# Two transformer blocks in fp32 on one core: evictions, weight halves and side work queued later

## What is computed

```python
def hybrid_mixer(h, pos, w_in, ...):
    z, xbc, dt_f, dt_b, q, k, v, gates = split_cols(h @ w_in, IN_SPLITS)
    xbc = silu(depthwise_centred_conv(xbc, conv_w, conv_b))          # 5 taps, 3072 channels
    xs, b_in, c_in = split_cols(xbc, (2048, 512, 512))
    ...
    y = ssd(xs, dtf, af, b_in, c_in) + flip(ssd(flip(xs), ...)) + d_skip * xs
    y = gated_group_rmsnorm(y, z, ssd_norm_g)                        # y * silu(z), 4 groups
    branch_ssd = y @ w_br_ssd
    q = rotary(q, pos); k = rotary(k, pos)
    branch_attn = windowed_gqa_with_sink(q, k, v, sink) @ w_br_attn  # 16 heads, window 128
    g_ssd, g_attn = split(sigmoid(gates))
    return (g_ssd * branch_ssd + g_attn * branch_attn) @ w_out
```

## Time and profile before

| what | value |
|---|---|
| median of three executions | 2611.15 us (2610.36 to 2611.34) |
| the profiled execution | 2610.12 us, its span 2608.3 us |
| TensorE busy | 2483.5 us (95%) |
| VectorE, ScalarE, GpSimd busy | 1327.3 us (51%), 929.5 us (36%), 477.9 us (18%) |
| mean granted TensorE clock | 0.981 |
| HBM traffic | 95 GB/s over the span |

### The profile page before, as it was taken

One profiled execution on the slowest core, in us unless ns is written; L12 is line 12 of the kernel. 1 busy time (PEld: TensorE's weight loads), 2 busy tenths in 40 slices (PEclk: granted clock), 3 DMA queues, 4 the chain that ended last, 5 costly groups with the idle time before them and its releaser, 6 DMA issues.

```text
span 2608.3 us, 29119 instructions
## 1 busy us (share of the span) xinstructions
PE 2483.5 (95%) x11378; PEld 1992.6 (76%) x11378; DVE 1327.3 (51%) x1957; ACT 929.5 (36%) x1488; POOL 477.9 (18%) x329
## 2 busy tenths in 40 slices
PE   6999899989789999999999999999999999999997
PEld 5766567867668788788888788888877787888886
DVE  3788855455776544444443344433477644444422
ACT  4334334233455433333332333322544333333321
POOL 2422100044330010111111111101355311111101
PEclk9999999989899999999999999999999999999998
DMA  5412123432344523233332233322321232333331
GB/s 162 124 57 57 41 89 135 140 97 77 101 138 143 196 97 113 73 97 97 97 97 97 81 103 97 98 97 95 93 65 57 73 113 64 92 98 97 98 102 49
DMA packets 173258, 254.20 MB, mean 97 GB/s; under 512 B 11840, under 2 KB 88896, under 8 KB 173120
## 3 DMA queue, kind: packets, MB, share of 16 engines
q1 hardware_dynamic: 173120, 252.33, 30.6%
HBM read 231.83 MB, written 16.78 MB: 95 GB/s over the span
## 4 chain that ended last, share of the span: by engine, by line
PE 76%; DVE 12%; issue 5%; ACT 4%; POOL 1%; DMA 1%; SPq 1%; DVEq 0%; ACTq 0%; POOLq 0%
PE bank L997 75%; DVE T L1716 3%; DVE W L1708 1%; POOL acc L2429 1%; ACT whi L1300 1%; DVE wlo L1708 1%; ACT pr L1392 1%; DVE pr L1712 1%; DVE T L1713 1%; DVE pr L1826 0%; PE bank L1077 0%; DMA scr_z<-T 0%; DVE SC L2343 0%; ACT T L1301 0%; DVE stg L1716 0%
## 5 line engine op out<-in xcount | busy, mean ns | idle before, releaser
L997 PE MATMUL bank<-xh,whi 128*128 128x512 f32 x1784 | 720.9, 404 | 22.0 <-DVE wlo L1708 17.6
L1708 DVE TENSOR_TENSOR wlo<-raw,whi 128x1024 fp32r<-128x1024 f32 (+1 forms) x354 | 438.9, 1243 | 570.9 <-ACT whi L1300 570.4
L997 PE MATMUL bank<-xh,wlo 128*128 128x512 f32 x1784 | 700.5, 393 | 0.0
L997 PE MATMUL bank<-xl,whi 128*128 128x512 f32 x1784 | 700.0, 392 | 0.0
L1300 ACT ACTIVATE whi<-raw 128x1024 fp32r<-128x1024 f32 (+2 forms) x406 | 416.5, 1038 | 541.6 <-PE bank L997 530.9
L997 PEld LDWEIGHTS bank<-xh,whi 128*128 128x128 f32 x1784 | 338.2, 190 | 119.5 <-issue 30.5
L997 PEld LDWEIGHTS bank<-xh,wlo 128*128 128x128 f32 x1784 | 337.5, 189 | 72.7
L997 PEld LDWEIGHTS bank<-xl,whi 128*128 128x128 f32 x1784 | 338.2, 190 | 69.3 <-issue 3.8
L997 PE MATMUL bank<-hh,wlo 128*128 128x512 f32 x528 | 205.6, 389 | 0.0
L997 PE MATMUL bank<-hl,whi 128*128 128x512 f32 x528 | 205.6, 389 | 0.0
L997 PE MATMUL bank<-hh,whi 128*128 128x512 f32 x528 | 205.6, 389 | 0.0
(11 more groups left out here) (341 smaller groups left out, 3623.5 us busy)
## 6 DMA issues: line engine op xcount, KB each, us to landing
raw<-in_w_in SPq DMA_DIRECT2D x92, 512.0 KB, 3.6
raw<-in_w_ffn_in SPq DMA_DIRECT2D x88, 256.0 KB, 3.3
raw<-in_ffn_gate SPq DMA_DIRECT2D x88, 256.0 KB, 2.8
raw<-in_ffn_up SPq DMA_DIRECT2D x88, 256.0 KB, 3.1
raw<-in_ffn_down SPq DMA_DIRECT2D x44, 512.0 KB, 3.5
raw<-in_w_ffn_out SPq DMA_DIRECT2D x22, 512.0 KB, 3.5
raw<-in_w_xattn_kv SPq DMA_DIRECT2D x16, 512.0 KB, 4.0
raw<-in_w_kv_mem SPq DMA_DIRECT2D x16, 512.0 KB, 3.8
```

Of the source, the lines that this page charges most:

```text
L997: return e.matmul(out, l, r, start=start, stop=stop, skip_group_check=skip)
L1708: return e.tensor_tensor(out, a, b, op)
```

## The change

- `gemm` no longer evicts a tile directly behind its matmuls: the eviction is put in `owed`, and paid behind the matmuls of the next tile, or at a mark, a drain or a flush.
- A slot's step is split in two: `w_hi` at the old place, `w_lo` put off with `soon(1, ...)` from the fourth slot on.
- `attention` is written anew: the evictions (`score_max`, `pt_out`, `o_out`), the shift, the exponentials and the normalisation are steps of their own, one yield or more behind what they read; its rate is 3.0 instead of 2.5.
- The copy of a turned tile (`turned`), the gates' tanh, z's product (`z_silu`), the square of the gated y (`z_square`) and the sums of the memories' squares (`m_sum`) are put off by `soon`.
- `y_add` stands first in its point. The states wait for the last read of the states of the group before (`off`, g-1, 3, 0) in place of the marks.
- The functions of the engines keep their operations; most are only renamed. The core of the diff:

```diff
@@ -308,10 +308,17 @@
 
         ORDER = []
         loaded, ready = [0], [0]
-        jobs, aged, beside, late, delayed, tails = [], [], [], [], [], []
+        jobs, aged, beside, late, delayed, tails, owed = [], [], [], [], [], [], []
 
         def step(kind, *args):
+            if kind == "mark":
+                pay()
             ORDER.append((kind, args))
+
+        def pay():
+
+            while owed:
+                owed.pop(0)()
 
         def load_to(j):
             while loaded[0] < min(j, NS):
...
@@ -321,7 +328,11 @@
         def split_to(j):
             while ready[0] < min(j, NS):
                 load_to(ready[0] + NR)
-                step("w", ready[0])
+                step("w_hi", ready[0])
+                if ready[0] < 4:
+                    step("w_lo", ready[0])
+                else:
+                    soon(1, "w_lo", ready[0])
                 ready[0] += 1
 
         def pump():
...
@@ -387,8 +403,9 @@
                     if j == 0:
                         main.new(name, m)
                     step("mm", name, j, m)
+                    pay()
                     if i == g["ids"][-1]:
-                        evict(m)
+                        owed.append(lambda m=m: evict(m))
                     if m == (g["M"] - 1) // 2:
                         pump()
                     run_beside((g["n"] if g["nat"] else g["ntok"]) / (4 * S))
...
@@ -491,31 +508,49 @@
             return max(n - 1, 0), min(n + 2, 4)
 
         def attention():
+
+
             for i in range(17):
+                here, last = i < 16, i - 1
+                k = keys(last)[1] - keys(last)[0] if i else 0
                 for pair in range(2):
-                    if i < 16:
-                        for r in (0, 1) if pair == 0 else (2, 3):
+                    if here:
+                        for r in (2 * pair, 2 * pair + 1):
                             side.new("sc", i, r)
                         step("scores", i, pair)
+                    if i > 1 and pair == 0:
+                        step("o_out", i - 2)
+                    if i and pair:
+                        step("pt_out", last, 0)
+                    yield
+                    if here:
+                        step("score_max", i, pair)
                         if pair:
-                            step("softmax", i)
-                        yield
-                    if i and pair == 0:
-                        k0, k1 = keys(i - 1)
-                        for j in range(k1 - k0):
-                            side.new("pt", i - 1, j)
-                            step("p_turn", i - 1, j)
-                            yield
-                    if i and pair:
-                        side.new("pv", i - 1)
-                        step("pv", i - 1)
-                    if pair and i < 16:
-                        step("p_norm", i)
-                    if pair:
-                        yield
+                            step("shift", i)
+                    if i:
+                        side.new("pt", last, pair)
+                        step("p_turn", last, pair)
+                    yield
+                if here:
+                    step("p_exp", i)
+                if i:
+                    step("pt_out", last, 1)
+                if k == 3:
+                    side.new("pt", last, 2)
+                    step("p_turn", last, 2)
+                    yield
+                    step("pt_out", last, 2)
+                yield
+                if i:
+                    side.new("pv", last)
+                    step("pv", last)
+                if here:
+                    step("p_norm", i)
+                yield
+            step("o_out", 15)
 
         step("mark", "qkv")
-        att = start(attention(), 2.5)
+        att = start(attention(), 3.0)
         step("conv_weights")
 
         def ev_conv(j):
...
@@ -534,6 +569,7 @@
                     def turn():
                         side.new("turn", j)
                         step("turn", j)
+                        soon(1, "turned", j)
                     return (lambda: turn()) if j < 20 else None
                 return silu
             jobs.append(conv)
...
@@ -542,7 +578,8 @@
             def evict(m):
                 tmp.new(key, base + m)
                 step("gate", key, base + m)
-                soon(1, "gate_out", key, base + m)
+                soon(1, "gate_tanh", key, base + m)
+                soon(2, "gate_out", key, base + m)
             return evict
 
         for g in range(4):
...
@@ -601,16 +638,19 @@
             g, c = posts.pop(0)
             z_there.discard((g, c))
             step("z_gate", g, c)
-            z_busy[0] -= 1
+
+            def square():
+                step("z_square", g, c)
+                z_busy[0] -= 1
+            soon(1, square)
             if c == 3:
-                soon(1, "y_mean", g)
-                soon(3, "y_scale", g)
+                soon(2, "y_mean", g)
+                soon(4, "y_scale", g)
 
 
         SEG, WITHIN, ELSE = (0, 1), (2,), (3,)
 
         def states(g):
-            step("mark", f"ssd{g}")
             for i in range(6):
                 if i == 0:
                     step("weigh", g, 0)
...
@@ -657,6 +697,10 @@
             ahead = groups(1, 4)
             for n in range(34):
                 for half in range(2):
+                    if half == 1 and n >= 2 and n % 2:
+                        step("y_add", (n - 2) // 2)
+                        if n % 8 == 1:
+                            posts.extend(((n - 2) // 8, c) for c in range(4))
                     if half == 0 and n >= 2:
                         if n % 2 == 0:
                             side.new("y", (n - 2) // 2, among=WITHIN)
...
@@ -672,10 +716,6 @@
                         step("decayed", n - 1)
                     if n % 8 >= 2:
                         next(ahead, None)
-                    if half == 1 and n >= 2 and n % 2:
-                        step("y_add", (n - 2) // 2)
-                        if n % 8 == 1:
-                            posts.extend(((n - 2) // 8, c) for c in range(4))
                     if posts and posts[0] in z_there:
                         post()
                     fetch_z()
...
@@ -686,7 +726,11 @@
                 tmp.new("z", g, m)
                 tmp.new("zt", g, m)
                 step("z_out", g, m)
-                z_done.add((g, m))
+
+                def silu():
+                    step("z_silu", g, m)
+                    z_done.add((g, m))
+                soon(1, silu)
             return evict
 
 
...
@@ -702,6 +746,7 @@
                 step("m_split", tag, k)
                 square(f"m{tag}", k)
                 soon(1, "m_lo", tag, k)
+                soon(1, "m_sum", tag, k)
                 yield
 
         def memory(tag):
...
@@ -735,8 +780,8 @@
                 step("y_turn", j)
                 if j < 15:
                     yield
-                if posts:
-                    fetch_z()
+                fetch_z()
+                if posts and posts[0] in z_there:
                     post()
             step("x_again")
 
...
@@ -1489,9 +1536,8 @@
                     return
                 to = c + 1 if d == 0 else c - 1
                 u, b = side("st", g, i)
-                w.wait_ge(*at("pe", f"ssd{g}"))
-                w.wait_ge(*at("dve", f"ssd{g}"))
-                w.wait_ge(*at("pool", f"ssd{g}"))
+                if g:
+                    w.wait_ge(*at("off", g - 1, 3, 0))
                 w.wait_ge(*at("state", g, i))
                 copy((HF, HB)[d][to][:], b[:]).then_inc(*up("h_first", ("h in", g, d, to), ("side", "free", u)))
 
...
@@ -2114,6 +2160,14 @@
                 w.wait_ge(*at("square", f"m{tag}", k))
                 stt(ml[tag][:, k, :], mt[tag][:, k, :], V("mem" if tag == 1 else "mem_2", k),
                     mh[tag][:, k, :].bitcast(F32), ALU.mult, ALU.subtract).then_inc(*up("m_lo", ("x lo", f"m{tag}", k)))
+
+            def m_sum(tag, k):
+                n, t = tmp("sq", f"m{tag}", k)
+                if k:
+                    w.wait_ge(*at("square", f"m{tag}", k))
+                    w.wait_ge(*at("sum", f"m{tag}", k - 1))
+                    tt(macc[:], macc[:], t[:, 0:256], ALU.add).then_inc(
+                        *up("sum", ("sum", f"m{tag}", k), ("tmp", "free", n)))
 
             def mk_out(tag, i, m):
                 n, t = tmp("mk_out", tag, i, m)
...
@@ -2500,8 +2554,8 @@
                     return
                 to = c + 1 if d == 0 else c - 1
                 H = (HF, HB)[d]
-                for other in ("pe", "dve"):
-                    w.wait_ge(*at(other, f"ssd{g}"))
+                if g:
+                    w.wait_ge(*at("off", g - 1, 3, 0))
                 w.wait_ge(*at("eto"))
                 w.wait_ge(*at("h in", g, d, c))
                 hs = slice(32 * d + 8 * g, 32 * d + 8 * g + 8)
```

## The result

The changed kernel takes 2615.78 us (median of 20 executions, 2610.47 to 2622.01) against 2610.56 us for the kernel before beside it (20 executions): a ratio of 1.0023, 95% interval 1.0016 to 1.0029. It is slower by 0.2%, where faster was forecast. The profiled execution took 2616.39 us, its span is 2614.6 us against 2608.3, and its mean granted clock 0.977 against 0.981.

The account below looks back on a forecast made before the run. TensorE was taken as the bound, with gains only where it has gaps: 2610.1 + 32 - 18 - 24 - 1 = 2599.1, with the median 1.0 us higher 2600 us; own range 2588 to 2612, with rivals 2568 to 2628.

Parts of the forecast that it names:

- The chain of rotations: Before attention: late low halves make the rotations serial, seven links, `xs0` near 125 us; +32 us, bounds 22 to 36.
- The rival without a chain: Rival: transfers overlap after all, so the change doesn't lengthen the rotations; 2568 us, chance 0.07.
- Attention: Attention stage: with VectorE's 19.2 us of waits gone it ends near 219 instead of 237; -18 us, between -25 and 0.
- VectorE idle for TensorE's scores by over 19 us: Sign, in attention, that would show the forecast wrong: VectorE standing idle that long for scores from TensorE.
- `turned` two tiles later: Attention: the late copy of a turned tile frees its bank later; a cost held inside the attention bound, -25 to 0.
- The scan: Scan stretches: three edits together cut 18 us of 42.8 idle and 6 of 28 lost to clock; -24 us, -55 to 0.
- `y_add`: Scan: queued ahead of a select and a decay product, it saves 9 us of TensorE's 15.3 us of waits for it.
- the first state copy: Scan: it no longer waits for VectorE's mark, which saves 4.5 us of TensorE's 5.4.
- Evictions a tile later: All stages: every eviction moves behind one more tile in its queue, no work added; 0, bounded by -2 and +3 us.
- The rest: Recurrence of the second mixer, after the scan: GpSimd's low halves block less; -1 us, between -4 and +3.
- The slower rival: Rival in the scan: late z transfers make ScalarE wait past some 25 us, taking the scan's gain; 2622 us, chance 0.28.
- score banks: Addition to the slower rival: they hold up TensorE and attention gives little; 2630 us.

Follow-up runs that it names:

- rot_halves_at_once: The changed kernel with the low halves of slots 4 to 17 made at once, later ones still put off: 2587.67 us, ratio 0.9902 to the kernel before.
- before_low_half_late: The kernel before with only the low halves from slot 4 on put off by two tiles: 2639.68 us, ratio 1.0107 to the kernel before.
- both mends: The changed kernel with low halves of slots 4 to 17 at once and score maxima queued in the scores' yield: 2573.75 us, ratio 0.9862 to the kernel before.

## Why the forecast missed, step by step

**The chain of rotations: right, in place and in what it costs.** Forecast were seven links of 7.6 us and `xs0` near 125; the trace has SP's transfers from 61.83 to 113.80 in seven links, 7.42 us each, and `xs0` at 123.52. The order load, transfer is there, the low half stands behind q by cos, and the experiments move the start of `xs0` by +28.9 us (after), +29.9 (put into the kernel before) and -27.1 (taken out). The rival without a chain, 2568, is out. One of the signs did not come: TensorE's gaps before `xs0` were to sum to 30 us more, and they grew by 19.3, from 23.1 to 42.4. The other 9.6 us of the +28.9 are TensorE's busy time, the same matmuls at a granted clock of 0.91 instead of 0.98. `xs0` waits for the end of the chain, so slow matmuls ahead of it fill time in which TensorE would have stood still.

VectorE's product by cos took 1.78 to 1.82 us in all eight rotations of q, each released by the same landing as GpSimd's product, and 0.68 for the first block of k, where it started first (45.72 against 45.95 us). That agrees with the Trainium skill (SBUF — State Buffer, "SBUF: two separate sides"), by which a VectorE operation with two inputs in SBUF and a GpSimd operation that reads SBUF exclude each other. The two were never apart in the chain, so what its rule would give back was not to be had.

**Attention: the step that failed.** I wrote that with the 19.2 us of waits gone the stage would end near 219 instead of 237. (My own figures do not quite give that: of VectorE's 36.3 us of idle time 17.1 would have been left, not 12 to 15.) The waits went, to 3.1, the stage got 3.6 us *longer*, and the stretch up to the branch gemm 5.5 us. The step from "VectorE is the slow one" to "VectorE's waits are the stage's" was wrong. VectorE has 195.7 us of work in 243.9, TensorE 221.2: neither is full, and each waits for the other, for scores, maxima and tiles. The time freed on VectorE went into waiting for TensorE (32.5 us, where it had been 7.1 for scores and tiles), as what TensorE needed did not come earlier. The text did name the cost, a bank that comes round after two yields with its maximum one yield in, but held it "inside the bound, since VectorE stays the limit". This was the term: 11 to 12 us, measured by moving the maximum alone. "VectorE idle for TensorE's scores by over 19 us" was my own sign of being wrong; it was 13.9 us for scores and 18.6 for tiles behind them. Without that delay the stretch is 352.6 us, 5.8 less than before: even then a third of the 18; the other 12 us are gain that the removed waits were to bring and did not. The clock was misjudged too. The forecast took 5 us off TensorE's 211 for it, and it went the other way: TensorE's idle time did fall by 3.3 us over the stretch, but its busy time rose by 8.8 for the same matmuls. That isn't the chain's doing: with the chain taken out (rot_halves_at_once) the stretch has 22.5 us idle and 339.9 busy. Behind two of the three waits for the maxima the clock looks like this (the waits end at 213.64 and 237.58 us, and were 4.1 and 4.2 us long):

```profile
213.00:220.00 7.00, 6.36 (x18) 4.78 (x19) 5.82 (x17) 2.17 (x9) 0.00 (x0) 0.52 0.26 77
236.00:244.00 8.00, 6.42 (x17) 4.55 (x18) 5.94 (x16) 2.60 (x9) 0.50 (x1) 0.57 0.22 66
```

The other cost named there, `turned` two tiles later, did not show.

**The scan: right, and a little small.** -29.0 against -24. Of TensorE's idle time 17.4 us went, where I took 18; the clock gave 12.1 us where I took 6. By parts: `y_add` about 6 us, not 9; the low halves about 11; evictions 4 or nothing; z's steps within 2; the first state copy nothing. TensorE's wait for it did fall from 5.4 to 2.8 us, but putting the mark back changes no time. All but the low halves are no larger than what chance does to this stretch, 5.9 us. The parts were measured in different kernels, and sum to 23 of the 29 at most.

**Evictions a tile later: the mechanism was missed.** I priced them at 0 (-2 to +3) by the bank that they hold longer. In the kernel after they give 14.8 us, 4.7 of it behind the scan. I looked only at what a late eviction holds, not at what moves ahead of it. In the rest the three kernels with late low halves and evictions at once took 1758.2 to 1761.0 us, 5.6 to 8.3 above the kernel before, and all others at most 1756.6; with both late, the kernel after is 0.9 above. So late evictions seem to pay there for the late low halves, but no kernel had late evictions without late low halves, and which wait goes was not taken apart. In attention the profiles have 4.8 us for them with the new order and 0.4 with the old.

**The rest** came to +0.9 against -1: right.

**The slower rival** named 2622 by z's transfers. The sign was right by luck, the cause wasn't: ScalarE waits some 10 us for scratch transfers in the scan after, most of it in this row of its waits,

```profile
ACT T L1348 <- DMA scr_z<-T: 9.7, 5, 3.1
```

far from the 25 us from which it was to decide, and with z's steps at once the kernel is not faster. The "score banks" that I set beside that rival are what happened. The forecast of 2600 missed by 16 us; in the profiles attention came out 23.5 us worse than its term and the rest 1.9, the scan 5.0 and the chain 3.1 better. It fell inside the range only because the rivals had widened it, past the forecast's own 2588 to 2612.

## What to carry to other kernels

When a step is put off in a list that feeds several in-order queues, follow it past everything that is issued between its old and its new place, DMA issues too: a low half moved behind a rotation cost 29 us, and issuing those few at once gave it back. Before a step is put off, ask who wants its result or its buffer, and how soon: the late maximum, whose bank is wanted two yields on, cost 12 us; the late normalisation, with its reader left in place, lengthened the stretch by 16.5; late evictions, whose banks are wanted four tiles on, gained 14.8 beside the other edits. In a stage where two engines both have slack and wait for each other, a removed wait may be worth nothing: look who waits next. And compare idle and busy time apart: in attention the idle time fell and the clock took more than that back.

## What the runs showed beside that

The clock weighs as much as the waits here, and it need not go their way. From before to after, the scan has 17.4 us less idle time and 12.1 less busy time for the same matmuls; the attention stretch has 3.3 less idle and 8.8 *more* busy, at a mean of 0.95 instead of 0.98. In the four kernels that share this stretch it has 22.5 to 22.7 us of idle time and 339.5 to 341.2 of busy time; before_low_half_late, with the attention of the kernel before, has 26.9 and 333.6. So this is hardly chance in one execution.

Over the whole span the share at the lower of the two levels, 2 x (1 - mean clock), is 99 us before (0.981), 120 after (0.977) and 77 with both mends (0.985). By an estimate that takes all of it as work at twice the time, half of the 43 us between the last two, some 21 us, is the clock's part of the 42 us between those kernels. TensorE's busy time says the same: 2494.1 us after, 2473.5 with both mends, 20.6 less.
